# Turning attention probabilities on Trainium2: a product with a diagonal matrix, or a division in place and a transposition

## What is computed

```python
sc = (jnp.einsum("bqhd,bkhd->bhqk", q[:, s:e], k[:, :e]) * scale
      + c[:, :, s:e, None] - c[:, :, None, :e])
causal = jnp.arange(s, e)[:, None] >= jnp.arange(e)[None, :]
p = jax.nn.softmax(jnp.where(causal, sc, MASK_VALUE), axis=-1)
outs.append(jnp.einsum("bhqk,bkhd->bqhd", p, v[:, :e]))
```

## Time and profile before

| | before |
|---|---|
| median of 3 runs | 2427.03 us (2426.28 to 2427.44) |
| span of the profiled execution | 2425.5 us |
| TensorE busy | 2390.9 us, 99% of the span |
| VectorE busy | 1435.7 us, 59% |
| ScalarE busy | 874.2 us, 36% |
| GpSimd busy | 1045.5 us, 43% |

### The profile page before, as it was taken

The page is one execution under the profiler, slowest core; times in us unless marked ns, Lnnn a source line. Parts: engine busy times, 40 slices in busy tenths (PEclk is TensorE's granted clock), DMA queues, the critical chain, the costliest instruction groups (busy, mean ns, idle before and its releaser), DMA issues.

```text
span 2425.5 us, 33627 instructions
## 1 busy us (share of the span) xinstructions
PE 2390.9 (99%) x11435; PEld 1464.0 (60%) x11435; DVE 1435.7 (59%) x2831; ACT 874.2 (36%) x1385; POOL 1045.5 (43%) x739
## 2 busy tenths in 40 slices
PE   8999899999999999999999999999999999999999
PEld 6888677658888875445454444444444466666665
DVE  4412455456867556544949894222222399999988
ACT  3222223232232242223135655544544433333332
POOL 0001111010000020000888888888888175578666
PEclk9999889999999999999999999999999999999999
DMA  7240100265656312942436666666666799999997
GB/s 207 70 72 1 53 10 10 70 178 156 191 176 205 87 53 70 345 174 87 87 48 153 154 148 153 155 147 154 155 147 156 257 401 375 370 361 375 374 361 287
DMA packets 437701, 426.49 MB, mean 176 GB/s; under 512 B 104809, under 2 KB 359913, under 8 KB 437489
## 3 DMA queue, kind: packets, MB, share of 16 engines
q1 hardware_dynamic: 353456, 332.85, 43.0%
q0 software_dynamic: 84160, 92.58, 15.5%
HBM read 364.28 MB, written 61.05 MB: 175 GB/s over the span
## 4 chain that ended last, share of the span: by engine, by line
PE 96%; DVE 2%; ACT 1%; SPq 0%; issue 0%; DMA 0%; POOL 0%; DVEq 0%; ACTq 0%; POOLq 0%
PE psum L1474 9%; PE psum L1475 9%; PE psum L1476 9%; PE psum L1499 7%; PE psum L1497 7%; PE psum L1498 7%; PE psum L1249 6%; PE psum L889 6%; PE psum L1206 5%; PE psum L1208 5%; PE psum L1207 5%; PE psum L1455 4%; PE psum L1106 1%; PE psum L1083 1%; PE psum L1062 1%; PE psum L1122 1%
## 5 line engine op out<-in xcount | busy, mean ns | idle before, releaser
L786 POOL DMA_INDIRECT dense_gates<-arena x384 | 607.2, 1581 | 151.6 <-issue 116.7
L1474 PE MATMUL psum<-arena 128*128 128x512 bf16 x1024 | 389.4, 380 | 0.0
L1476 PE MATMUL psum<-arena 128*128 128x512 bf16 x1024 | 387.1, 378 | 0.0
L1475 PE MATMUL psum<-arena 128*128 128x512 bf16 x1024 | 386.6, 378 | 0.0
L2545 DVE TENSOR_TENSOR arena<-arena,psum 128x1024 bf16<-128x1024 f32 x124 | 151.5, 1221 | 352.2 <-ACT psum L1855 351.7
L1498 PE MATMUL psum<-arena,low 128*128 128x384 bf16 x1024 | 333.8, 326 | 0.0
L1499 PE MATMUL psum<-arena,low 128*128 128x384 bf16 x1024 | 333.8, 326 | 0.0
L1497 PE MATMUL psum<-arena,low 128*128 128x384 bf16 x1024 | 333.8, 326 | 0.0
L1871 ACT ACTIVATE low<-low 128x1024 bf16<-128x1024 f32 x128 | 135.3, 1057 | 296.3 <-PE psum L1499 282.6
L814 POOL DMA_INDIRECT arena<-gelu_spill,arena x128 | 178.3, 1393 | 87.5 <-DMA gelu_spill<-cst 43.3
L806 POOL DMA_INDIRECT arena<-in_v,arena x128 | 166.3, 1300 | 103.0 <-DVE arena L2592 77.5
(11 more groups left out here) (377 smaller groups left out, 3937.0 us busy)
## 6 DMA issues: line engine op xcount, KB each, us to landing
arena<-in_uT SPq DMA_DIRECT2D x128, 512.0 KB, 4.6
low<-in_v SPq DMA_DIRECT2D x128, 512.0 KB, 5.3
gelu_spill<-cst SPq DMA_DIRECT2D x128, 256.0 KB, 3.4
arena<-in_ada_w POOLq DMA_DIRECT2D x12, 2048.0 KB, 9.3
dense_gates<-arena SPq DMA_DIRECT2D x4, 6144.0 KB, 40.1
arena<-gelu_spill SPq DMA_DIRECT2D x128, 192.0 KB, 5.2
arena<-dense_gates SPq DMA_DIRECT2D x128, 192.0 KB, 6.7
low<-in_w_in SPq DMA_DIRECT2D x20, 1024.0 KB, 7.4
```

The costliest lines, as they stand in the source:

```text
L786: pool.indirect_dma_start(gate_cells, bass.IndirectOffsetOnAxis(ap=cell_of[:, n:n + 1], axis=0), gate_of[:, n:n + 1], None, compute_op=ALU ...
L1474: mm(psum[:, bank, :], hi[:, c, :], h2hi[:, c, :], start=c == 0, stop=False)
L1475: mm(psum[:, bank, :], hi[:, c, :], h2lo[:, c, :], start=False, stop=False)
L1476: last = mm(psum[:, bank, :], lo[:, c, :], h2hi[:, c, :], start=False, stop=c == DC - 1)
```

## The change

Instead of a diagonal matrix, VectorE multiplies the probabilities themselves, in place in `sc`, by the reciprocal (16 to 128 rows, 128 to 528 columns). TensorE turns each block by a transposition with the identity as the moving operand. The two buffers `dg` go away, and with them the norm's wait for the turn two steps earlier. No instruction is added, removed or moved in VectorE's, ScalarE's, GpSimd's or SyncE's program, and on TensorE 120 products become 120 transpositions at the same places. Behind line 237 the line numbers are one less, and behind the norm three less.

```diff
-        dg = carve(2, P)
...
                 for j in range(m + 1):
                     kr = P if j < NT - 1 else LAST
-                    last = mm(psum[0:kr, 1, j * rows:(j + 1) * rows], sc[s % RING_S][0:rows, j * P:j * P + kr],
-                              dg[0:rows, s % 2, 0:rows], start=True, stop=True)
+                    last = pe.transpose(psum[0:kr, 1, j * rows:(j + 1) * rows], sc[s % RING_S][0:rows, j * P:j * P + kr],
+                                        const("ident")[0:rows, 0:rows])
                 last.then_inc(S["x_t"], 1)
...
             def attend_norm(s):
                 h, m, rows, keys = fox(s)
                 col = rs[0:rows, s % RING_S:s % RING_S + 1]
+                a = sc[s % RING_S][0:rows, 0:keys]
                 dve.wait_ge(S["x_exp"], s + 1)
-                if s >= 2:
-                    dve.wait_ge(S["x_t"], s - 1)
                 settle(dve.reciprocal(col, col))
-                dve.tensor_scalar(dg[0:rows, s % 2, 0:rows], const("ident")[0:rows, 0:rows], col, None, ALU.mult
-                                  ).then_inc(S["x_nrm"], 1)
+                dve.tensor_scalar(a, a, col, None, ALU.mult).then_inc(S["x_nrm"], 1)
```

## The result

| kernel | median us | lowest to highest | runs |
|---|---|---|---|
| before | 2426.66 | 2419.34 to 2427.44 | 4 |
| changed | 2407.97 | 2406.20 to 2408.89 | 4 |

The profiled execution of the changed kernel took 2407.0 us from first to last instruction, before it was 2425.5. (A run's device time stands 1.8 us above its span: 2408.77 for this one.)

The account below looks back on a forecast made before the run. TensorE, busy 99% of the span, was taken as the bound. TensorE's saving of -14.3 us plus +3.7 us of waits gave -10.6 us, from 2427.0 to 2416.4 us, range 2409 to 2429.

Parts of the forecast that it names:

- The sign and the mechanism: Whole kernel: TensorE, busy 99%, is the bound, so less TensorE work makes it faster; over 0.2% faster had 0.67.
- The full blocks: First attention's turns on TensorE: 80 blocks of 128 rows save 0.11 us each, 8.8 us.
- The thin blocks: Turns of m = 4: 40 blocks of 16 rows save 0.11 us each, 4.5 us; better end 0.16 each, 6.3 us.
- The waits: First attention: turns waiting for the longer norm, and savings lost in earlier waits, give back +3.7 us, between 1 and 8.
- VectorE and the collision: First attention: longer norms add 5 us of VectorE, mostly hidden; meeting GpSimd's masking a little more often stays inside +3.7.
- The removed wait: Norm's wait for the turn two steps earlier: that turn is already over, so no gain and no loss.
- The output weights: Their load, issued 13.5 us before first use: the distance shrinks by at most 1 us; costed at 0.
- the clock: First attention: work saved in stretches at 1.2 GHz counts nearly double, 1.0 us more, up to 1.8.
- those that fell: Clock rivals in the first attention: a full fall, 2434 us, chance 0.13; a partial fall, 2425 us, chance 0.15.
- the clock falls less: Rival: the low-clock stretch from 300 to 340 us is escaped, giving 2408 us; chance 0.08.
- The rival of the falling clock: First attention: thin work becomes a larger share, so the clock falls more often; 2434 us, chance 0.13 (partial: 2425, 0.15).

Follow-up runs that it names:

- turn_only: Kernel before with blocks turned by transpositions; the scaled diagonal is still made but unread, so the division is left out: 2408.26 us, ratio 0.9923.
- no_divide: Changed kernel without VectorE's multiplication by the reciprocal, so the division is left out: 2409.62 us, ratio 0.9937 to the kernel before.
- wait_back: Changed kernel with the norm's removed wait for the turn two steps earlier put back: 2406.57 us, ratio 0.9926 to the kernel before.
- norm_only: Changed kernel with blocks turned by products with the identity again, probabilities still divided in place: 2427.80 us, ratio 1.0000 to the kernel before.
- large_only: Changed kernel with transpositions only for the 80 full blocks; the 40 blocks of 16 rows use products with the identity: 2421.94 us, ratio 0.9984.
- thin_more: Changed kernel with each 16-row block transposed three times into the same place: 2416.95 us, ratio 0.9973 to the kernel before.
- The fillers: Six products nobody reads, ahead of TensorE's waits at 264, 276 and 279 us: 2400.86 us in the changed kernel, 2414.52 in the kernel before.
- before_fill: Kernel before with six products nobody reads ahead of three TensorE waits: 2414.52 us, ratio 0.9950.

## Why the prediction was right and wrong

**The sign and the mechanism held.** TensorE is the bound, and work taken off it counts. The changed kernel is faster by over 0.2%, which had 0.67.

**The full blocks** were priced at 0.11 us each from a row of transpositions elsewhere in the kernel. Measured: 0.115.

**The thin blocks were mis-sized.** "With half the records I take off 0.11 each" gave 4.5 us; it was 0.15 each, 6.1 us. The row that had it right was in the text, four transpositions of 16 rows in 0.42 us, kept as the better end. A transposition's time follows its rows more than its records, and a row of the very shape should have beaten the count of records. This cost 1.6 us of the miss.

**The waits were right in size, not in place.** +3.7 was forecast and +3.0 measured as idle time. By turn_only (0.5 to 3.0 us) and no_divide (2.4 to 3.6) the norm's own share is about that or less. I had put small waits of 0.25 to 0.34 in nine places; there are four waits, of 0.5 to 0.7 us. The two kinds of place are right (328.52 is a step without an item, 339.95 one after a step without a Y), but most of the nine show none, so that the sum came near is in part luck. Why those had slack I didn't test.

**VectorE and the collision.** +5 us was forecast for the norm and +6.1 came; time in which norms are held up by GpSimd rose from 1.0 us (my 0.6 left out the norms of 16 rows) to 1.9. I had not thought of other instructions: the 16-column additions pay 3.8 us more and the maskings 3.1. The Trainium skill's rule on the shared pair of ports (SBUF — State Buffer, "SBUF: two separate sides"), by which I had worked out 3.6 us for the norms, gave too much for them, as my reading of the trace of before gave too little. For all of VectorE's instructions in the stage it is some 6.5 us now (1.9 on the norms, 4.6 on the small additions), against 1.9 before. None of it shows beyond the +3.0 of waits, so the term that held it, "inside the +3.7", was large enough.

**The removed wait** was worth nothing, as forecast (wait_back).

**The output weights** came near to being late, but weren't. They are issued from 415.54 and first used at 426.17, a distance of 10.6 us where it was 13.5; it shrank by 2.9, and I had allowed for 1. The timelines, and how long the first two issues (the part that the first use needs) took to land:

```profile
415.54 5.99 SPq L498 DMA_DIRECT2D low<-in_w_out  x4
...
426.17 3.60 PE L1048 MATMUL psum<-arena,low 128*128 128x512 f32 x8
...
DMA to landing us min/median/max: 5.0/6.6/8.2
```

The 5.99 us are the time over which the four issues are spread, not the loading. The later of the first two is issued at 415.96 and lands 8.2 us behind, at 424.1, so 2.0 us were left, where the kernel before had 5.7.

**The step that failed is the clock.** The sum treated it as given, with "1.0" for the work that stood in its lower stretches, and moved every doubt about it into rivals, of which those that fell had 0.28 together and "the clock falls less" had 0.08. It came true: 5.1 us in the stage where the sum had 1.0, and 1.7 behind it, which are luck. The term was mis-sized by 4 us in the stage, the largest part of the miss of 8. Over all runs the mean clock went from 0.9905 to 0.9928, which by 1.9 us for each 0.001 is 4.4 us; at equal clock the change is worth 12 to 14 us (the table by clock), near the 10.6 of the forecast once the thin blocks are priced right. So the clock is a quarter to a third of the gain. I had read the evidence: thin instructions stand before the fall. But I drew it the wrong way. I argued that less full work leaves a larger share of thin work. The thin turn, 1.13 us long, was itself halved and more, to 0.37, and where it stays long (norm_only, large_only, thin_more) the mean clock stays at 0.990. That it is the reason is likely and not shown: the profiles of these three have no fall at 310 us either, but a long one at 280, as the changed kernel has. I named this in half a sentence, "the turns of m = 4, thin themselves, are halved too", and gave it no weight. The range's lower end took in only "part of the luckier clock".

The rival of the falling clock is not borne out: the changed kernel has 27.3 and 20.5 us at the lower clock in its two profiles where the kernel before has 37.6, and the kernel with nothing but the transpositions (turn_only) has 13.6. The Trainium skill's statement behind it, that a transposition doesn't count as busy for the clock as a product does (TensorE: Matmul & The Clock Gate, "Part 4: PE-mode transpose"), is not refuted by this, since groups of five are short; but 240 records of products turned into 120 of transpositions didn't lower the clock here.

**Open:** why executions of one kernel land on mean clocks from 0.988 to 0.994 with the same work, and what exactly in a run of thin work brings the clock down. The fillers show that the falls at 263 and 280 us hang on TensorE's waits; for the fall behind thin work the kernels show neither a certain cause nor a fixed place.

## What to carry to other kernels

Where TensorE is the bound and its clock is not always granted, price a change twice, in work and in clock, and look at which thin or idle stretch the change shortens just before a fall: here the clock was a quarter to a third of the gain. Compare kernels at equal mean clock before believing a difference of a few us, look whether the profiled run is like the others, and expect two halves of a change not to add when one is the cover of the other. A wait of TensorE that can't be removed may be worth filling with products that nobody reads.

## What the runs showed of the hardware

- Work that is thrown away made the kernel faster: six products of 128x512, 5.9 us of TensorE, brought 8.3 us (2409.18 to 2400.86), all of it through the granted clock.
- The clock can also fall with TensorE hardly idle: 29.91 of 30 us busy and a mean clock of 0.72 (before_fill, one run of five), with a run of 16x16 items and a turn of ten 16-column records ahead of it.
- Transposing a 128x128 block of float32 takes half the time of a product with the identity, 0.11 us of 0.22, and 16 rows of it 0.07 (0.37 for five) of 0.23 (1.13 for five). The product's time hardly depended on the width of the moving operand (128 or 16 columns) while the stationary one had 128 columns; the transposition's did. With both at 16x16 a product took 0.05 us (302.85 to 302.90 in before_fill).
- A VectorE addition of 0.16 us that began within GpSimd's masking took 1.05 us and ended with it; the masking took 1.70 in place of 1.09 where a VectorE addition of 128x512 ran in its first part. Against the kernel before VectorE lost some 4.5 us more and GpSimd 3.1 in the stage to such meetings, brought about by a shift between the engines.
- VectorE's multiplication by a column took 482 ns for 16x528 and 486 for 128x512: the rows are free and the columns count.
